# Attention units with signals for each half of the heads, and scores and mask products regrouped

## The reference

```python
m = jnp.maximum(jnp.max(s, axis=-1, keepdims=True), sink)
p = jnp.exp(s - m)
p = p / (jnp.sum(p, axis=-1, keepdims=True) + jnp.exp(sink - m))
```

## Time and profile before

| | us |
|---|---|
| three runs | 1654.16, 1657.45, 1658.60 (median 1657.45) |
| the profiled execution, its own time | 1656.64 |
| its span, from the first to the last instruction | 1654.8 |
| busy: PE / DVE / ACT / POOL | 1617.8 / 988.4 / 626.8 / 640.9 |
| NSA attention on PE | 541.6 to 702.0 of the span |
| SWA attention on PE | 1157 to 1235.5 of the span |

### The profile page before, as it was taken

One profiled execution on the slowest core, in us unless ns is written; L12 is line 12 of the kernel. 1 busy time (PEld: TensorE's weight loads), 2 busy tenths in 40 slices (PEclk: granted clock), 3 DMA queues, 4 the chain that ended last, 5 costly groups with the idle time before them and its releaser, 6 DMA issues.

```text
span 1654.8 us, 20967 instructions
## 1 busy us (share of the span) xinstructions
PE 1617.8 (98%) x8074; PEld 1271.4 (77%) x8074; DVE 988.4 (60%) x1363; ACT 626.8 (38%) x1225; POOL 640.9 (39%) x417
## 2 busy tenths in 40 slices
PE   8999999999999999999999999999899999999998
PEld 6888667677888666688888888888558888888886
DVE  7987255567835677637555564457853655556444
ACT  4222334434723666533222232334553322222323
POOL 3444311054422332244444444444334544444442
PEclk9999999999999999999999999999999999999998
DMA  7222201042211000023222223223002223233221
GB/s 256 101 90 102 77 20 45 14 186 95 95 65 64 14 2 2 2 76 102 89 102 100 92 102 104 101 88 103 27 1 89 96 96 102 90 102 97 94 102 51
DMA packets 37812, 133.81 MB, mean 81 GB/s; under 512 B 4753, under 2 KB 5201, under 8 KB 37201
## 3 DMA queue, kind: packets, MB, share of 16 engines
q1 hardware_dynamic: 35840, 125.71, 22.2%
q10 hardware_dynamic: 1872, 6.75, 1.1%
HBM read 130.35 MB, written 2.10 MB: 80 GB/s over the span
## 4 chain that ended last, share of the span: by engine, by line
PE 87%; issue 4%; DVE 4%; ACT 2%; POOL 1%; DMA 1%; ACTq 0%; DVEq 0%; POOLq 0%
PE ps L1599 18%; PE ps L1600 18%; PE ps L1601 18%; PE ps L2000 5%; PE ps L2001 5%; PE ps L2002 4%; PE ps L1920 3%; PE ps L1954 3%; PE ps L1935 3%; ACT sb_arena L730 1%; PE ps L1656 1%; PE ps L1686 1%; PE ps L1924 1%; PE ps L1708 1%; POOL sb_w_lo L432 1%
## 5 line engine op out<-in xcount | busy, mean ns | idle before, releaser
L432 POOL TENSOR_TENSOR sb_w_lo<-sb_raw,sb_w_hi 128x1024 fp32r<-128x1024 f32 x226 | 554.8, 2455 | 814.5 <-ACT sb_w_hi L460 789.0
L1599 PE MATMUL ps<-sb_x_hi,sb_w_hi 128*128 128x512 f32 x1368 | 536.5, 392 | 2.2 <-DVE sb_arena L1396 1.8
L1601 PE MATMUL ps<-sb_x_hi,sb_w_lo 128*128 128x512 f32 x1368 | 532.5, 389 | 0.0
L1600 PE MATMUL ps<-sb_x_lo,sb_w_hi 128*128 128x512 f32 x1368 | 532.3, 389 | 0.0
L460 ACT CAST sb_w_hi<-sb_raw 128x1024 fp32r<-128x1024 f32 x226 | 237.8, 1052 | 651.7 <-PE ps L1601 479.0
L1599 PEld LDWEIGHTS ps<-sb_x_hi,sb_w_hi 128*128 128x128 f32 x1368 | 256.8, 188 | 59.2 <-issue 2.9
L1600 PEld LDWEIGHTS ps<-sb_x_lo,sb_w_hi 128*128 128x128 f32 x1368 | 256.9, 188 | 53.7 <-issue 1.2
L1601 PEld LDWEIGHTS ps<-sb_x_hi,sb_w_lo 128*128 128x128 f32 x1368 | 256.8, 188 | 53.6
L1436 DVE TENSOR_TENSOR sb_x_lo<-sb_arena,sb_x_hi 128x512 fp32r<-128x512 f32 x44 | 98.3, 2240 | 104.5 <-ACT sb_x_hi L788 104.5
L2002 PE MATMUL ps<-sb_x_hi,sb_w_lo 128*128 128x512 f32 x336 | 130.7, 389 | 0.0
L2000 PE MATMUL ps<-sb_x_hi,sb_w_hi 128*128 128x512 f32 x336 | 130.7, 389 | 0.0
(11 more groups left out here) (284 smaller groups left out, 1864.6 us busy)
## 6 DMA issues: line engine op xcount, KB each, us to landing
sb_raw<-in_w SPq DMA_DIRECT2D x227, 512.0 KB, 3.2
sb_arena<-in_cmp_w1k ACTq DMA_DIRECT2D x1, 2048.0 KB, 9.5
sb_arena<-in_cmp_w1v ACTq DMA_DIRECT2D x1, 2048.0 KB, 15.4
out<-sb_resid SPq DMA_DIRECT2D x8, 256.0 KB, 2.3
sb_resid<-in_x SPq DMA_DIRECT2D x4, 256.0 KB, 6.6
sb_resid<-in_x ACTq DMA_DIRECT2D x4, 256.0 KB, 7.4
sb_arena<-in_pool_w SPq DMA_DIRECT2D x1, 1024.0 KB, 11.9
sb_arena<-in_invc SPq DMA_DIRECT2D x1, 1024.0 KB, 13.9
```

What stands on the lines that cost most here:

```text
L432: nc.gpsimd.tensor_tensor(WL[:, w % SPL], raw[:, w % RAW], WH[:, w % SPL].bitcast(F32), ALU.subtract).then_inc(tile_split, 1)
L1599: mm(out, WH[:, s, k], XH[:, k], start=(k == 0), stop=False)
L1600: mm(out, WH[:, s, k], XL[:, k], start=False, stop=False)
L1601: ins = mm(out, WL[:, s, k], XH[:, k], start=False, stop=(k == KT - 1))
```

## The change

All in the attention units; the linear layers stay.

- `nmax`, `p_exp` and `pt_mm` count halves instead of units: in NSA the DVE makes the maxima as two instructions, one for each half, each with a signal; ACT waits for its half's maxima, and signals after each half's exponentials; PE signals after each half's transposes. In SWA the maxima stay one instruction for both halves (`maxima_done` counts them).
- `turn` waits for half hh's exponentials and half hh's copy of the unit before, just ahead of half hh's transposes. The DVE's copy waits for half 0's transposes alone.
- `score` makes the score products of both pairs first, and then one mask product for each half (two in SWA from i = 1 on) that spans both pairs: its output has the pairs as a dimension with a stride, and its moving operand is the mask tile read again for each pair (stride 0). The second pair's score product no longer has `start=True`; the first one's does it for the bank.

```diff
+def maxima_done(v):
+    return 2 * v + 2 if v < len(NSA_UNITS) else len(NSA_UNITS) + v + 1
...
                 def exps(v):
-                    act.wait_ge(nmax, v + 1)
                     if v >= 2:
-                        act.wait_ge(pt_mm, v - 1)
+                        act.wait_ge(pt_mm, 2 * (v - 1))
...
                     for hh in range(2):
+                        act.wait_ge(nmax, maxima_done(v) if swa else 2 * v + hh + 1)
                         for r in range(pairs):
                             ins = nc.scalar.activation(PE_[:, v % 2, hh, n * r:n * (r + 1)],
...
-                    ins.then_inc(p_exp, 1)
+                        ins.then_inc(p_exp, 1)
                 def evac(v):          # ACT
-                    act.wait_ge(pt_mm, v + 1)
+                    act.wait_ge(pt_mm, 2 * v + 2)
...
                     if not swa:       # DVE, maxima
-                        nc.vector.tensor_reduce(low, s_, AX.X, ALU.max, negate=True).then_inc(nmax, 1)
+                        for hh in range(2):
+                            nc.vector.tensor_reduce(low[:, hh], s_[:, hh], AX.X, ALU.max, negate=True).then_inc(nmax, 1)
...
                 def evac(v):          # DVE
-                    dve.wait_ge(pt_mm, v + 1)
+                    dve.wait_ge(pt_mm, 2 * v + 1)
                 def weight(v):
-                    dve.wait_ge(p_exp, v + 1)
+                    dve.wait_ge(p_exp, 2 * v + 2)
...
                 def score(v):         # PE
-                        pe.wait_ge(p_exp, v - 1)
+                        pe.wait_ge(p_exp, 2 * (v - 1))
...
+                    s_ = [PS[:, 2 + 2 * (v % 2) + hh, 0:n * pairs].rearrange("p (r n) -> p r n", r=pairs) for hh in range(2)]
                     for r in range(pairs):
-                        s_ = [PS[:, 2 + 2 * (v % 2) + hh, n * r:n * (r + 1)] for hh in range(2)]
                         for hh in range(2):
                             half = slice(DH * hh, DH * hh + DH)
-                            mm(s_[hh], QN[half, c + r, P * i:P * (i + 1)], K[half, k0:k0 + n], start=True, stop=False)
-                        for hh in range(2):
-                            if swa and i >= 1:
-                                mm(s_[hh][:, 0:P], identb[:], masks[:, 2], start=False, stop=False)
-                            ins = mm(s_[hh][:, n - P:n], identb[:], masks[:, 1], start=False, stop=True)
+                            mm(s_[hh][:, r], QN[half, c + r, P * i:P * (i + 1)], K[half, k0:k0 + n], start=(r == 0), stop=False)
+                    masked = lambda x: masks[:, x].unsqueeze(1).broadcast_to([P, pairs, P])
+                    for hh in range(2):
+                        if swa and i >= 1:
+                            mm(s_[hh][:, :, 0:P], identb[:], masked(2), start=False, stop=False)
+                        ins = mm(s_[hh][:, :, n - P:n], identb[:], masked(1), start=False, stop=True)
                     ins.then_inc(s_mm, 1)
                 def turn(v):
-                    pe.wait_ge(p_exp, v + 1)
-                    if v >= 1:
-                        pe.wait_ge(pt_d, v)
-                        pe.wait_ge(pt_a, v)
                     for hh in range(2):
+                        pe.wait_ge(p_exp, 2 * v + hh + 1)
+                        if v >= 1:
+                            pe.wait_ge(pt_a if hh else pt_d, v)
                         for n in range(pairs * len(key_tiles(i, swa))):
                             ins = nc.tensor.transpose(PS[:, 6 + hh, P * n:P * (n + 1)], PE_[:, v % 2, hh, P * n:P * (n + 1)],
                                                       ident[:])
-                    ins.then_inc(pt_mm, 1)
+                        ins.then_inc(pt_mm, 1)
```

More of the change, by code:

```diff
@@ L1355, in maxima @@
                     nc.vector.tensor_tensor(low, nmx[:, v % 4, :, 0:pairs], sink, ALU.min).then_inc(nmax, 1)
-                    dve.wait_ge(nmax, v + 1)
+                    dve.wait_ge(nmax, maxima_done(v))
                     nc.vector.tensor_tensor(ske[:, v % 4, :, 0:pairs], low, sink, ALU.subtract).then_inc(qb_raw, 1)
```

## The result

| us | before | after |
|---|---|---|
| median of four executions | 1657.03 (1654.16 to 1658.60) | 1634.85 (1634.42 to 1638.14) |
| the profiled execution, its own time | 1656.64 | 1638.14 |
| its span | 1654.8 | 1636.3 |
| first score product of NSA | 541.56 | 543.78 |
| NSA, from there to the next layer's first product | 160.18 | 147.07 |

The account below looks back on a forecast made before the run. PE was taken to bound the kernel, stalled in attention by a chain through DVE and ACT. Gains 2.8 + 8.5 + 3.1 + 1.7 = 16.1 us gave 1640.5, or 1641.3 for the median; range 1636 to 1650.

Parts of the forecast that it names:

- the term of 2.8 us for scores and masks: PE's score units in both stages each 0.10 us shorter: 1.6 us in NSA and 1.2 in SWA.
- the hidden stalls: Late turns in NSA that don't show as idle, 0.21 to 0.29 us each, 4.3 us in sum, all expected to go.
- the clock drop at SWA's end: Half clock on PE after the last turn's long wait; expected to go, for 1.7 us.
- The rival of slow wide masks: 88 wide mask products take 0.44 us each instead of 0.11, so PE pays 29 us: 1670.3 us; chance 0.04.
- Halves in NSA: NSA turns: 4.3 us hidden stalls plus 4.9 idle waits, less 0.7 that stays, 8.5 us gained.
- The added claim that the 0.44 us of transposes that go ahead would have covered these stalls: NSA turns: half 0's four transposes going ahead, 0.44 us, alone exceed every hidden stall of 0.2 to 0.3 us.
- The bound above of 9.2: Largest gain from halves in NSA, 9.2 us, if none of the idle waits stays.
- 1.1 + 0.16 - 0.4: NSA's last idle wait: 1.1 us shown plus 0.16 not shown, of which some 0.4 stays.
- Halves and clock in SWA: SWA turns: 3.1 us from half 0's transposes going ahead, and 1.7 from the clock drop at the stage's end going.
- Waits and signals: The 64 added waits inside turns and the added signals from PE and ACT cost 0; a wait's upper bound was 0.11 us.
- Lost on the way: Rival: the chain doesn't hold the turns, or saved time is lost at the next layer's start; 1651 us, chance 0.10.
- The forecast's variants: Whole kernel: the forecast with its clock variants, 1637 to 1645 us for the bounds of mask product and waits; chance 0.72.

Follow-up runs that it names:

- e9_twice: The changed kernel with the score products of NSA's two-pair units made twice into the same banks; NSA 155.79 us in a single execution.
- e1_scores: The kernel before with only the score part of the change, no halves; 1651.45 us, ratio 0.996, stages NSA 157.33, SWA 76.07.
- e2_halves: The changed kernel with scores and mask products in the old order, all half signals kept; 1645.34 us, ratio 0.9921, stages NSA 150.66, SWA 73.79.
- e3b_narrow: The changed kernel with narrow mask products for each half and pair behind all scores, instead of wide ones; 1637.98 us, ratio 0.9885.
- e4_maxwhole: The changed kernel with NSA's maxima as one instruction for both halves again; 1641.62 us, ratio 0.9902, NSA 150.45.
- e5_turnwhole: The changed kernel, but each turn waits ahead of its first transpose for both halves' exponentials and copies; 1643.08 us, ratio 0.9914.
- e10_both_five: Repeat of e8_both, without edit, beside the changed kernel on one chip; 1635.38 us, ratio 0.987, SWA 68.39.
- e8_both: The changed kernel with SWA's maxima by halves too and ACT's copy ahead of the next unit's exponentials; 1634.27 us, ratio 0.9862, SWA 68.40.
- after_five: The changed kernel run again without edit; 1637.35 us, ratio 0.988, stages NSA 147.07, SWA 72.81.
- e7_copy_first: The changed kernel with ACT's copy of a unit's half 1 ahead of the next unit's exponentials, both stages; 1636.71 us, ratio 0.9874, SWA 70.03.

## Why the prediction was right or wrong

**The step that failed is the price of the score passes**, in the term of 2.8 us for scores and masks. The mechanisms were right: the switch from masks back to scores went, the hidden stalls went, and so did the clock drop at SWA's end. The prediction counted "four passes in a row, 4 x 0.32 = 1.28, for the second pair's first pass loads its weights behind the first pair's second one as that did behind the first". The 0.32 of the earlier trace rows is the distance from the first pass of a run to the second, and from the last to the mask; both have something extra. In the middle of a run a pass costs 0.216, as the unit at 573.52 and e9_twice (0.87 for four) show; e1_scores and e2_halves show that the saving follows this part of the change, with the halves and without. Worked again from before's start times, a second pair costs 0.32 + 0.32 us plus 0.21 from the first masks to its first pass; in after it costs 2 x 0.216. The masks cost 0.11 more, as forecast. So a unit is 0.64 + 0.21 - 0.43 - 0.11 = 0.31 shorter, not 0.10. The term of 2.8 us measured 6.1 on top of the halves (e2_halves against after) and 5.2 alone. Over 28 units it would be 8.7. The rest was taken back by the chain, which is late again where PE has become faster: in SWA the pair of units is 0.31 us shorter than in e2_halves and not 0.62, and in NSA the turns at i = 0 hold waits.

So the whole miss of 6.5 us is made up thus: 3.3 from this term (6.1 in place of 2.8), 1.0 from the halves in NSA, -0.2 from halves and clock in SWA, 2.0 by which the medians of four differ more than the stages do, and 0.4 from the base (the forecast started from a median of 1657.45, and the fourth execution brought it to 1657.03).

**Masks.** Taken at 0.11 us each of 256 columns, measured 0.12 and 0.11. The rival of slow wide masks is out; e3b_narrow shows that the wide form does nothing either way.

**Halves in NSA.** Forecast 8.5, measured 9.5 alone (e2_halves). Hidden stalls of 0.2 to 0.3 us a pair were there and went, as the start times had said: turns at i = 1 to 3 stand at their mask's pitch (all but the first at i = 1, which has a wait inside, and the last), and the pace of a pair at i = 2 and 3 goes from 5.60 and 6.84 to 5.28 and 6.58. The added claim that the 0.44 us of transposes that go ahead would have covered these stalls is half right: e4_maxwhole shows it for i = 3, and shows that the faster score part needs the rest at i = 1. The bound above of 9.2 was 0.3 too low. By the turns' start times, 0.6 of the 1.0 us more than forecast lies from the second to last turn on (6.89 us to the next layer in e2_halves, 8.34 before: 1.45 less, where 1.1 + 0.16 - 0.4 was counted), and the rest at i = 2 and 3. The stage's last turn and its second unit are still late, as forecast.

**Halves and clock in SWA.** Forecast 3.1 + 1.7, measured 4.6 together (e2_halves). The drop at the end went and the early one stayed, as taken; e1_scores and e5_turnwhole tie it to the turn by halves, for with whole turns it is there. Its price can be estimated from start times: before takes 6.44 us from the last turn's first transpose to the next layer (1229.03 to 1235.47), and after 4.27 from the last turn's second half (1213.23 to 1217.50), to which the other half's 0.44 is added; 6.44 - 4.71 = 1.7, as forecast. That leaves 2.9 for the halves against 3.1. The steady pair of units, with the old scores, goes from 8.64 to 8.18, where 0.44 was counted. The early drop isn't worth 1.7, though: e10_both_five has none (its clock is 1.00 over all of SWA), and its stage takes 68.39 us against 68.40 in e8_both, which has one of 3.4 us. These are single executions.

**Waits and signals.** Both taken at 0, and right. Eight transposes with a signal and a wait in their middle take 0.88 us (647.78 to 648.66), as before. The Trainium skill's rule of 26 ns for each increment on completion ("TensorE: Matmul & The Clock Gate", "The cost: per-tile semaphore tail") doesn't show on PE's stream here; that section fits the tail behind a group of tiles, which no run here isolates.

**Lost on the way.** Nothing was, as far as can be seen: the stretch between the stages stayed at 455.33 us, and the one behind SWA (418.84 against 419.37) inside the scatter of 417.6 to 420.0 of all profiles.

**The range.** The forecast's variants reached down to 1637, from 1641.3 less the bounds of the mask product; the price of a pass had no bound at all, though the trace of before holds one. V products of the same 256 columns, two side by side as the scores are, start there at 574.38, and the scores behind them at 575.40. Seen pass by pass they are 0.27, 0.22, 0.21 and 0.32 us apart:

```profile
574.65 0.60 PE L1954 MATMUL ps<-sb_arena 128*64 128x256 f32 x4
574.87 0.60 PE L1954 MATMUL ps<-sb_arena 128*64 128x256 f32 x4
575.08 0.39 PE L1954 MATMUL ps<-sb_arena 128*64 128x256 f32 x2
```

With 0.216 for the two middle distances of the scores, as one end of a range, the term would have had 28 x 2 x 0.10 = 5.8 us more room and the range would have begun near 1630. As the forecast itself it would have given 1635.5. That this is so near the measured 1634.9 would have been luck in part, since only 6.1 of the 8.7 us came through and the halves and the scatter gave more than was counted. Against the median of all twelve executions, 1636.2, the range from 1636 would just have held.

## What to carry to other kernels

The distance between two instructions has a price for the kind of change between them as well as for the instructions: take the price of a longer run from the middle of a run, and count each switch between half-array and whole-array products, both ways. When two lengths of a loop are nearly equal, a saving in one shows only in part until the other is cut too (in NSA 2.85 us alone and 3.6 on top of the halves). Compare stages by their start times: NSA repeated to 0.1 us where the kernel's own time scattered by 5. And look at a wait both as idle time and as the length that a group is drawn with, for a wait in the middle of a group of products hardly shows as idle.

## What the hardware showed that was not expected

- A run of float32 products of 64 rows, halves side by side, goes at 0.216 us per pass of 256 columns in its middle. Its first distance is 0.32, and so is the one from its last pass to a whole-array product. The way back, from the second mask to a score pass, took 0.15 us where a narrow mask alone takes 0.06. The Trainium skill ("TensorE: Matmul & The Clock Gate", "The mechanism") lets a weight load be pulled ahead of running products when it goes to other rows or to the background buffer. The middle of a run agrees: in the run from 573.52, the load for the third pass (starting at 574.05) begins at 573.84, and in the units at i = 0 passes of 128 columns stand 0.11 apart, in proportion, so nothing is left over for loads. At the switch to the masks, the load begins only at 574.58, together with its product at 574.59. The 0.10 at both ends thus goes with a load that isn't ahead. That it is the cause wasn't tested, and the section has no price for it.

```profile
573.84 0.19 PEld L1926 LDWEIGHTS ps<-sb_arena 64*128 64x128 f32 x2
...
574.58 0.11 PEld L1931 LDWEIGHTS ps<-sb_masks,sb_identb 128*128 128x128 bf16 x2 [0.33 <-issue]
```

- The same program (e8's) reached one point of its work at 541.08 us in one execution and at 543.78 in another.
- The clock drop in the query part is 3.4 us long in most profiles, but in after_five 0.83 over 20 us makes 6.8 us at half clock, and the stage was 1.5 us longer with it than in after. e7_copy_first had one of 6.8 us too, and e5_turnwhole and e10_both_five had none there.
